# The mixer's heads between the steps of its projections on TensorE

## The chip, the cores and the metric

The kernel runs on one core of one Trainium2 chip. Its time is the device time of one launch in microseconds (us), the median over a few launches. The engines are TensorE (PE, with its weight loads as PEld), VectorE (DVE), ScalarE (ACT), GpSimd (POOL) and SyncE (SP, which issues the weight loads from memory). Each runs its own list of instructions strictly in order; semaphores order them against each other.

## The reference

Two transformer blocks on 512 tokens of width 1024 in fp32. The first block is a feed-forward part, a token mixer and a second feed-forward part, all scaled and shifted by a modulation vector; then come two layers with attention. The change touches the token mixer alone:

```python
def token_mix(y, w_in, conv_w, conv_b, gate_b, mnorm_g, lb, hnorm_g, w_out):
    p = y @ w_in                              # 1024 x 4104: mq mk mv mo | mif (8) | hq hf hi hg, 512 each
    mq, mk, mv, mo, mif, hq, hf, hi, hg = split(p)
    mq, mk = split(silu(causal_dwconv(concat(mq, mk), conv_w, conv_b)))    # 4 taps
    log_i, log_f = mif + gate_b, then log_sigmoid of the second half
    hm = mlstm_chunkwise(q, k, v, log_i, log_f)          # 4 heads of 128
    out_m = head_rmsnorm(hm, mnorm_g) * sigmoid(mo)
    fgate = lb + (1 - lb) * sigmoid(hf)
    ho = hgrn2_chunkwise(silu(hq), 1 - fgate, hi, log(fgate))              # 4 heads of 128
    out_h = head_rmsnorm(ho, hnorm_g) * silu(hg)
    return concat(out_m, out_h) @ w_out
```

`mlstm_chunkwise` is, per head, h = (W * (q k^T)) v over a normaliser, with W[t,s] = exp of differences of running sums of the gates, causal. `hgrn2_chunkwise` is a linear recurrence with a decay for each channel: o[t] = sum over s <= t of (q[t] * k[s] * decay(s..t)) summed over channels, times v[s].

## The kernel before

Activations lie feature-major: 128 features on the partitions, 512 tokens along the free axis. A product `y @ w` runs in **halves**: 128 output columns, 8 steps over the contraction (k), and 3 matmuls a step (`passes`), since both operands are split into a high and a low part of type fp32r: high by high, low by high, high by low. A half is thus 24 matmuls of 512 columns into one PSUM bank. The weights come in units of two halves through `raw` (2 slots, a `dma_start` on SP each). ACT copies a half to its high part (`split_hi`, into `wh`), DVE subtracts for the low part (`split_lo`, into `wl`); both run four halves ahead of PE. The products for `v` and `hi` are taken token-major instead (`token_major`), with 256 columns a matmul and one half for two halves' weights.

The mixer (`mix` on each engine) has three stretches:

1. The input product: 17 units, 33 tiles (the unit `if` has 8 columns), in the order of the table `MIX`. ACT evicts each tile and applies silu or sigmoid on the way; for q and k it copies to SBUF (`tmpB`), DVE convolves there and ACT applies silu.
2. The heads. First the four mLSTM heads ("M" below). For each key tile j: PE makes scores (L1736), DVE the argument of the weights from a row that PE has spread over the partitions (L1730, L1251), ACT their exponential (L794), POOL the causal edge (L569), DVE the product (L1258), PE values and row sums (L1747, L1749). At the head's end come an exponential and an absolute value on ACT, a maximum, a reciprocal (L1264) and a product on DVE, then a square on ACT, a mean over the head on PE (`head_stat`, L1696), a reciprocal root on ACT, gain and gate on DVE, and the split into high and low parts. Then the four HGRN heads ("H"): running sums (L1191), and for each of nine **levels** a subtraction on DVE (L1301), two exponentials on ACT (L812, L813), two products into `pair` on DVE (L1313, L1314), 4 matmuls of 128 columns on PE (L1769) and a masked copy of their result on DVE (L1284). The matmuls of the heads are plain fp32, and the profile shows two records for each.
3. The output product: 4 units, 8 halves over the eight head outputs, which all must be there first (`product`).

The attention layers further on are already written in another manner: PE's list takes steps of a product (a generator `beside`) between the matmuls of the attention, a fixed number at each place (`more(n)`).

## Time and profile before

| | us |
|---|---|
| Median of 3 runs | 2939.34 (2937.59 to 2943.41) |
| The profiled execution, its own time | 2942.35 |
| Its span, first to last instruction | 2940.5 |
| PE busy in the span | 2608.4 (89%) |
| DVE, ACT, POOL busy | 1417.3, 979.2, 216.1 |
| Mixer: input product | 493 to 677 |
| Mixer: heads | 677 to 951 |
| Mixer: output product | 951 to 997 |

Busy time is read with the granted clock of TensorE beside it (PEclk, 1.00 is 2.4 GHz and 0.50 is 1.2 GHz): matmuls at the lower level take twice as long and make PE look busier than its work is. A matmul's duration contains its way through the array, which overlaps the next one; what one costs in a row of them is the distance between two starts.

### The profile page before, as it was taken

Reading aid. Unit: us, or ns where it says so; the run is one execution under the profiler, and the core shown is the slowest. Engines: PE = TensorE matmul, PEld = TensorE weight load, DVE = VectorE, ACT = ScalarE, POOL = GpSimd, SP = SyncE. Lnnn points to the kernel's source line nnn. Section 1 sums busy time; section 2 is a strip of 40 time slices with the busy share of each in tenths; the row PEclk is TensorE's granted clock in tenths of the full one; section 3 lists DMA queues with packets and bytes.
Section 4 is the critical chain, followed back from the end, with each engine's and each line's share of the span. In section 5 each row is a group of like instructions: output and inputs, shape, how many; then the busy total and the mean of one; then the engine's idle time right before and its main releaser. Section 6 shows DMA issues by size and latency. Waiting matters only on the chain. (4 is left out here: it accounts for less than half of the span.)

```text
span 2940.5 us, 28742 instructions
## 1 busy us (share of the span) xinstructions
PE 2608.4 (89%) x11468; PEld 2035.1 (69%) x11468; DVE 1417.3 (48%) x2200; ACT 979.2 (33%) x1515; POOL 216.1 (7%) x199
## 2 busy tenths in 40 slices
PE   2899898996656899999898899999799988999997
PEld 1788786883344688887676678888576545788875
DVE  5676524524555433322544375532655553755325
ACT  2322224332222432323333433322434443333233
POOL 0000110000000100001200110001210002000011
PEclk9999999997666999999999999999999998999999
DMA  8365423650000132322222123322132101333221
GB/s 286 126 194 193 148 90 58 90 111 30 0 0 0 43 113 89 100 90 83 84 82 78 44 86 101 100 97 95 61 99 68 56 29 43 101 100 101 97 83 57
DMA packets 229204, 257.73 MB, mean 88 GB/s; under 512 B 7208, under 2 KB 218664, under 8 KB 229072
## 3 DMA queue, kind: packets, MB, share of 16 engines
q1 hardware_dynamic: 218624, 221.30, 25.0%
q0 software_dynamic: 8672, 31.43, 3.4%
q10 hardware_dynamic: 1776, 3.18, 0.3%
q8 instruction: 91, 1.49, 0.2%
q14 instruction: 41, 0.34, 0.0%
HBM read 251.66 MB, written 2.62 MB: 86 GB/s over the span
## 5 line engine op out<-in xcount | busy, mean ns | idle before, releaser
L1049 DVE TENSOR_TENSOR wl<-raw,wh 128x1024 fp32r<-128x1024 f32 (+1 forms) x398 | 478.3, 1205 | 1024.7 <-ACT wh L616 1024.0
L1586 PE MATMUL G<-yh,wh 128*128 128x512 f32 x1928 | 776.9, 403 | 61.1 <-DVE yl L1079 26.0
L616 ACT ACTIVATE wh<-raw 128x1024 fp32r<-128x1024 f32 (+1 forms) x398 | 412.1, 1038 | 1106.4 <-PE G L1586 1067.4
L1586 PE MATMUL G<-yl,wh 128*128 128x512 f32 x1928 | 758.5, 393 | 0.0
L1586 PE MATMUL G<-yh,wl 128*128 128x512 f32 x1928 | 758.1, 393 | 0.0
L1586 PEld LDWEIGHTS G<-yh,wh 128*128 128x128 f32 x1928 | 367.0, 190 | 169.9 <-issue 54.3
L1586 PEld LDWEIGHTS G<-yl,wh 128*128 128x128 f32 x1928 | 366.2, 190 | 78.6
L1586 PEld LDWEIGHTS G<-yh,wl 128*128 128x128 f32 x1928 | 366.9, 190 | 77.3 <-issue 4.2
L1586 PE MATMUL G<-hidh,wh 128*128 128x512 f32 x704 | 280.7, 399 | 0.0
L1586 PE MATMUL G<-hidl,wh 128*128 128x512 f32 x704 | 278.9, 396 | 0.0
L1586 PE MATMUL G<-hidh,wl 128*128 128x512 f32 x704 | 278.8, 396 | 0.0
L512 POOL TENSOR_TENSOR acc<-acc,tmpC 128x512 f32<-128x512 f32 x86 | 148.0, 1721 | 961.8 <-ACT tmpC L622 961.8
L1586 PEld LDWEIGHTS G<-hidh,wl 128*128 128x128 f32 x704 | 132.9, 189 | 32.7 <-issue 1.0
L1586 PEld LDWEIGHTS G<-hidh,wh 128*128 128x128 f32 x704 | 132.9, 189 | 32.5 <-issue 1.0
L1586 PEld LDWEIGHTS G<-hidl,wh 128*128 128x128 f32 x704 | 132.7, 189 | 32.0
L692 ACT ACTIVATE hidh<-tmpA 128x512 fp32r<-128x512 f32 x88 | 55.6, 632 | 215.6 <-DVE tmpA L1146 215.6
L1586 PE MATMUL G<-wh,yh 128*128 128x256 f32 x384 | 114.2, 297 | 0.9 <-DVE aq L1334 0.9
L1586 PE MATMUL G<-wl,yh 128*128 128x256 f32 x384 | 108.7, 283 | 0.0
L1586 PE MATMUL G<-wh,yl 128*128 128x256 f32 x384 | 108.7, 283 | 0.0
L1769 PE MATMUL X<-pair 128*128 128x128 f32 x224 | 53.6, 416 | 53.2 <-DVE pair L1314 52.8
L1149 DVE TENSOR_TENSOR hidl<-tmpA,hidh 128x512 fp32r<-128x512 f32 x88 | 60.9, 693 | 61.4 <-ACT hidh L692 61.4
L1769 PEld LDWEIGHTS X<-pair 128*128 128x128 f32 x224 | 46.5, 308 | 60.0 <-issue 51.8
(263 smaller groups left out, 2929.4 us busy)
## 6 DMA issues: line engine op xcount, KB each, us to landing
raw<-in_ffn_w_in SPq DMA_DIRECT2D x44, 1024.0 KB, 5.1
raw<-in_ffn_w_gate SPq DMA_DIRECT2D x22, 1024.0 KB, 5.4
raw<-in_ffn_w_up SPq DMA_DIRECT2D x22, 1024.0 KB, 5.4
ada_c<-in_ada_w POOLq DMA_DIRECT2D x22, 1024.0 KB, 5.6
raw<-in_ffn_w_down SPq DMA_DIRECT2D x16, 1024.0 KB, 5.0
raw<-in_w_in SPq DMA_DIRECT2D x16, 1024.0 KB, 9.6
raw<-in_ffn_w_out SPq DMA_DIRECT2D x16, 1024.0 KB, 5.0
raw<-in_na_w_qkv SPq DMA_DIRECT2D x12, 1024.0 KB, 5.1
```

The source lines that it names most:

```text
L512: nc.gpsimd.tensor_tensor(acc[:, :], acc[:, :], C2[:, n % 2, :], ALU.add)\
L616: nc.scalar.activation(place(wh), src, ACT.Copy).then_inc(hi, 1)
L692: nc.scalar.activation(hidh[:, 2 * j + i, :], A2[:, i, :], ACT.Copy).then_inc(hidh_ready, 1)
L1049: nc.vector.tensor_tensor(place(wl), src, f32(place(wh)), ALU.subtract).then_inc(lo, 1)
L1149: nc.vector.tensor_tensor(hidl[:, 2 * j + i, :], A2[:, i, :], f32(hidh[:, 2 * j + i, :]), ALU.subtract).then_inc(hid_ready, 1)
L1586: ins = nc.tensor.matmul(bank, a, b, start=first and i == 0, stop=last and i == 2)
L1769: ins = nc.tensor.matmul(bank[:, c], a, b, start=True, stop=True)
```

## The change

The heads move from a stretch of their own in between the steps of the two products. The heads' work is cut into 64 **slots**: an H head has 10, an M head 5, in the order H0 H1 M0 M1 H2 H3 M2 M3, and 4 slots follow the last head. ACT, DVE and PE each walk the same table `SLOTS`. In a slot of an H head, PE takes 4 steps of a product (12 matmuls) and one level; in a slot of an M head, 4 steps, one score matmul, and one key tile's values. From slot 54 on fewer steps are left. What ends a head (`finish`, table `FIN`) lies in the up to four slots behind it. The columns of the input product are reordered (`MIX`), so that the first H heads' columns come first: 6 halves run before slot 0, 27 beside slots 0 to 53, and the first two halves of the output product, taken head by head, from slot 54 on; its other 6 follow as before. The weight splits and evictions of a half stand in every second slot (`block_behind`). Every head writes its values to bank G2 and the products use G0 and G1.

The convolution reads the PSUM bank directly (`conv`), in four operations on DVE with the bias in the first, and no copy by ACT goes ahead of it. The gates' and activations' silu and sigmoid are taken in place in five batches (`batched`, at slots 9, 24, 39, 49 and 55), since each change of function set needs an ACT_TABLE_LOAD; the gating of the head outputs is held back to slots 50 to 63 (`GATE_SLOT`).

```diff
-        MIX = (("q", 0), ("q", 1), ("k", 0), ("k", 1), ("v", 0), ("v", 1), ("if", 0),
-               ("hf", 0), ("hf", 1), ("hq", 0), ("hq", 1), ("hi", 0), ("hi", 1),
-               ("mo", 0), ("mo", 1), ("hg", 0), ("hg", 1))
+        MIX = (("hf", 0), ("hq", 0), ("hi", 0), ("q", 0), ("k", 0), ("v", 0), ("if", 0), ("hf", 1), ("hq", 1),
+               ("hi", 1), ("q", 1), ("k", 1), ("v", 1), ("hg", 0), ("hg", 1), ("mo", 0), ("mo", 1))
...
+        HEADS = (("H", 0), ("H", 1), ("M", 0), ("M", 1), ("H", 2), ("H", 3), ("M", 2), ("M", 3))
+        SLOTS = []
+        FIN = {}
+        for z, (kind, x) in enumerate(HEADS):
+            for i in range(LEVELS + 1 if kind == "H" else TT + 1):
+                SLOTS.append((z, kind, x, i))
+            for f in range(4):
+                FIN.setdefault(len(SLOTS) + f, []).append((z, kind, x, f))
+        SLOTS += 4 * [(8, "", 0, 0)]
+        BESIDE = [b for b in range(6, 34) if b != 13]
...
+        GATE_SLOT = {50: ("H", 0), 51: ("H", 1), 52: ("H", 2), 53: ("H", 3), 56: ("M", 0), 57: ("M", 1),
+                     59: ("M", 2), 63: ("M", 3)}
+        O_ORDER = list(GATE_SLOT.values())
...
+                def block(b, kind, half, t, g):
+                    if kind not in ("v", "hi"):
+                        split_hi(b + 4)
+                    if kind == "if":
+                        split_hi(b + 5)
+                    if kind in "qk":
+                        return
+                    act.wait_ge(done, b + 1)
+                    bank, c = G[BANK[g]], 2 * half + t
+                    if kind in ("v", "hi"):
+                        token_rows(mv if kind == "v" else hv, half, t, g)
+                        if t:
+                            split_hi(b + 3)
+                            split_hi(b + 4)
...
+                def batched(s):
+                    if s == 9:
+                        evicted(act, mix_of("k", 0))
+                        evicted(act, mix_of("k", 1))
+                        todo = [(mqk[:, n, :], ACT.Silu) for n in (0, 4, 1, 5)]
+                    elif s == 24:
+                        todo = [(hk[:, 2, :], ACT.Sigmoid), (hk[:, 3, :], ACT.Sigmoid), (hq[:, 2, :], ACT.Silu),
+                                (hq[:, 3, :], ACT.Silu)]
...
+                    for ap, fn in todo:
+                        ins = nc.scalar.activation(ap, ap, fn)
+                    ins.then_inc(batch, 1)
+                    log_and_exp()
...
+                for s, (z, kind, x, i) in enumerate(SLOTS):
+                    if i == 0:
+                        for of in FIN.get(s, ()):
+                            finish(*of)
+                    if kind == "H" and i < LEVELS:
+                        level_exp(x, i + 1)
+                    if kind == "M" and i < TT:
+                        weight_exp(x, i)
+                    if i:
+                        for of in FIN.get(s, ()):
+                            finish(*of)
+                    if block_behind(s):
+                        block(*block_behind(s))
...
+                def conv(b, n, g):
+                    dve.wait_ge(done, b + 1)
+                    w = vec[:, VOFF["conv_w"] + 4 * n:VOFF["conv_w"] + 4 * n + 4]
+                    bias = vec[:, VOFF["conv_b"] + n:VOFF["conv_b"] + n + 1]
+                    bank = G[BANK[g]]
+                    st.do(nc.vector.tensor_scalar(mqk[:, n, :], bank[:, :], w[:, 3:4], bias, ALU.mult, ALU.add))
+                    for d in (1, 2):
+                        st.do(nc.vector.scalar_tensor_tensor(mqk[:, n, d:S], bank[:, 0:S - d], w[:, 3 - d:4 - d],
+                                                             mqk[:, n, d:S], ALU.mult, ALU.add))
+                    nc.vector.scalar_tensor_tensor(mqk[:, n, 3:S], bank[:, 0:S - 3], w[:, 0:1], mqk[:, n, 3:S],
+                                                   ALU.mult, ALU.add).then_inc(gfree[BANK[g]], 1)
...
+                for s, (z, kind, x, i) in enumerate(SLOTS):
+                    fins = FIN.get(s, ())
+                    if i == 0 and s and HEADS[z - 1][0] == "H":
+                        for of in fins:
+                            finish(*of)
+                        fins = ()
+                    if kind == "H":
+                        if i:
+                            level_mul(x, i)
+                        elif z:
+                            level_sums(z, x)
+                        if i < LEVELS:
+                            level_sub(x, i + 1)
                         if i == 1:
...
+                            if z:
+                                dve.wait_ge(nd_mm, z)
+                            st.do(nc.vector.memset(attD, 0.0))
+                        if i:
+                            level_copy(x, i - 1)
+                    if kind == "M":
+                        if i < TT:
+                            weight_arg(x, i)
+                        if i:
+                            weight_scores(z, x, i - 1)
+                    for of in fins:
+                        finish(*of)
+                    if block_behind(s):
+                        block(*block_behind(s))
+                    rows(s)
+                    if s == 25:
+                        dve.wait_ge(batch, 2)
+                        forget_gate(2)
+                        forget_gate(3)
+                    if s in GATE_SLOT:
+                        gate_o(s)
+                    if s - 1 in GATE_SLOT:
+                        low_o(s - 1)
...
+            def beside_mixers():
+                for x in BESIDE:
+                    b, kind, g = b0 + x, MIX[x // 2][0], mix_tile(x // 2, x % 2)
+                    if kind in ("v", "hi"):
+                        yield from token_major_steps(b, g, x % 2, yh, yl)
+                        continue
+                    pe.wait_ge(lo, b + (2 if kind == "if" else 1))
+                    bank_free(pe, g)
+                    for k in range(KT):
+                        ins = passes(G[BANK[g]][:, :], wh[:, b % 4, k, :], wl[:, b % 4, k, :], yh[:, k, :],
+                                     yl[:, k, :], k == 0, k == KT - 1)
+                        if k == KT - 1:
+                            ins.then_inc(done, 2 if kind == "if" else 1)
+                        yield
+                b, g = BB["mixo"], TB["mixo"]
+                for n, (kind, x) in enumerate(O_ORDER):
+                    k = o_tile(kind, x)
+                    pe.wait_ge(o_ready, n + 1)
+                    for i in range(2):
+                        s = (b + i) % 4
+                        if n == 0:
+                            pe.wait_ge(lo, b + i + 1)
+                            bank_free(pe, g + i)
+                        ins = passes(G[BANK[g + i]][:, :], wh[:, s, k, :], wl[:, s, k, :], moh[:, k, :], mol[:, k, :],
+                                     n == 0, n == KT - 1)
+                        if n == KT - 1:
+                            ins.then_inc(done, 1)
+                        yield
...
+                for s, (z, kind, x, i) in enumerate(SLOTS):
+                    n = 2 if s < 54 else 1 if s < 62 else 0
+                    if kind == "H":
+                        more(2 * n)
+                        level(x, i)
+                    elif kind == "M":
+                        if i == 0:
+                            pe.wait_ge(batch, 3 if x >= 2 else 1)
+                            if x:
+                                pe.wait_ge(em_ready, x)
+                            else:
+                                pe.wait_ge(uT_ready, 1)
+                            gate_row(x, mo[0:4, 3, :]).then_inc(mb_mm, 1)
+                        if i < TT:
+                            scores(x, i)
+                        more(n)
+                        if i >= 2:
+                            ins = values(z, x, i - 2)
+                        more(n)
+                        if i == TT:
+                            values(z, x, TT - 1).then_inc(nd_mm, 1)
+                            gate_row(x, mrow[0:4, :]).then_inc(mt_mm, 1)
...
-            product("mixo", 3, 8, yh, yl)
+            product("mixo", 3, 8, moh, mol, 2)
```

How the lists stand. PE before, at the end of the M heads and through one H head (X and G are PSUM banks, `pair` the operands of a level, `att` the finished weights):

```order
L1753 MATMUL X<-pair,cst 128x512
L1696 MATMUL G<-tmpC,onesH 128x512
L1769 MATMUL X<-hq,hk 128x128 x4
L1769 MATMUL X<-pair 128x128 x28
L1772 MATMUL X<-pair 128x128 x2
L1776 MATMUL X<-pair 128x256 x2
```

PE after, at the end of slot 0 and the start of slot 1 of the first H head (L1771 are the three matmuls of a product step):

```order
L1771 MATMUL G<-yh,wh 128x512
L1771 MATMUL G<-yh,wl 128x512
L1771 MATMUL G<-yl,wh 128x512
L1949 MATMUL X<-hq,hk 128x128 x4
L1771 MATMUL G<-yh,wh 128x512
```

Levels that followed each other directly now have 12 product matmuls ahead of each.

DVE before, two levels of an H head (subtraction, two products, masked copy):

```order
L1301 TENSOR_TENSOR tmpC<-tmpB 128x512
L1313 TENSOR_TENSOR pair<-hk,tmpC 128x128x2
L1314 TENSOR_TENSOR pair<-hq,tmpC 128x128x2
L1284 COPY_PREDICATED att<-lev,X 128x512
L1301 TENSOR_TENSOR tmpC<-tmpB 128x512
L1313 TENSOR_TENSOR pair<-hk,tmpC 128x64x4
```

DVE after, slot 2 of the first H head and the start of slot 3 (L1161 is the low part of a weight half, L1312 to L1316 the convolution):

```order
L1360 TENSOR_TENSOR pair<-hk,tmpC 128x128x2
L1361 TENSOR_TENSOR pair<-hq,tmpC 128x128x2
L1347 TENSOR_TENSOR tmpC<-tmpB 128x512
L1371 COPY_PREDICATED att<-lev,X 128x512
L1161 TENSOR_TENSOR wl<-raw,wh 128x1024
L1312 TENSOR_SCALAR mqk<-G,vec 128x512
L1314 SCALAR_TENSOR_TENSOR mqk<-G,vec,mqk 128x511
L1314 SCALAR_TENSOR_TENSOR mqk<-G,vec,mqk 128x510
L1316 SCALAR_TENSOR_TENSOR mqk<-G,vec,mqk 128x509
L1360 TENSOR_TENSOR pair<-hk,tmpC 128x64x4
```

The masked copy has moved behind the subtraction, and in every second slot a weight half's low part, and in eight slots a convolution, stand between one level's subtraction and its products.

ACT after, slots 24 and 25 (L881 a batch, L663 the return to the exponential's set, L844 and L845 the end of head M0, L834 the weights of M1):

```order
L781 ACTIVATE hv<-G 128x2x256
L881 ACT_TABLE_LOAD
L881 ACTIVATE hk<-hk 128x512 x2
L881 ACT_TABLE_LOAD
L881 ACTIVATE hq<-hq 128x512 x2
L663 ACT_TABLE_LOAD
L844 ACTIVATE rstd<-X 128x512
L845 ACTIVATE tmpA<-G 128x512
L834 ACTIVATE tmpC<-tmpB 128x512
```

The end of a head waits on ACT behind three table loads and four activations.

## Rows read from the trace of the kernel before

**Rows 1.** Busy time of each engine by stretch: three mixer stretches, one attention layer.

```profile
core 0: us, PE busy (x) PEld busy (x) DVE busy (x) ACT busy (x) POOL busy (x), PEclk, DMA share, GB/s
493.00:677.00 184.00, 183.93 (x984) 159.47 (x983) 69.28 (x81) 69.60 (x92) 0.00 (x0) 0.99 0.53 92
677.00:951.00 274.00, 155.04 (x480) 102.56 (x480) 149.72 (x266) 65.90 (x138) 4.67 (x16) 0.63 0.01 4
951.00:997.00 46.00, 45.97 (x194) 37.34 (x194) 8.58 (x7) 14.86 (x21) 12.23 (x7) 0.97 0.23 69
2180.00:2436.00 256.00, 226.76 (x983) 144.12 (x984) 138.25 (x323) 102.62 (x219) 3.22 (x6) 0.93 0.16 52
```

**Rows 2.** PE in order of time (start, duration): last input and first output matmul.

```profile
676.54 0.39 PE L1586 MATMUL G<-yl,wh 128*128 128x512 f32 x1
...
951.03 0.80 PE L1586 MATMUL G<-yh,wh 128*128 128x512 f32 x1 [4.34 <-DVE yl L1183]
```

**Rows 3.** PE in order of time: one level's four matmuls at the upper clock.

```profile
823.56 1.05 PE L1769 MATMUL X<-hq,hk 128*128 128x128 f32 x8
```

**Rows 4.** PE in order of time, second attention layer: product steps and fp32 matmuls.

```profile
2206.22 0.39 PE L1586 MATMUL G<-yh,wl 128*128 128x512 f32 x1
...
2207.83 0.39 PE L1586 MATMUL G<-yl,wh 128*128 128x512 f32 x1
2208.15 1.13 PE L1967 MATMUL X<-ak,aq 64*128 64x512 f32 x4
2209.21 0.50 PE L1586 MATMUL G<-yh,wh 128*128 128x512 f32 x1
...
2213.54 3.70 PE L1986 MATMUL G<-PT,av 128*128 128x512 f32 x8 [0.84 <-ACT PT L892]
```

**Rows 5.** DVE in order of time: the cadence of two levels.

```profile
841.00 0.72 DVE L1284 COPY_PREDICATED att<-lev,X 128x512 f32<-128x512 uint8 x1
841.61 0.68 DVE L1301 TENSOR_TENSOR tmpC<-tmpB 128x512 f32<-128x512 f32 x1
843.08 0.43 DVE L1313 TENSOR_TENSOR pair<-hk,tmpC 128x256 f32<-128x256 f32 x1 [0.79 <-ACT tmpC L813]
843.42 0.42 DVE L1314 TENSOR_TENSOR pair<-hq,tmpC 128x256 f32<-128x256 f32 x1
```

**Rows 6.** ACT in order of time: the exponentials between them.

```profile
842.32 0.42 ACT L812 ACTIVATE tmpC<-tmpC 128x256 f32<-128x256 f32 x1 [2.03 <-DVE tmpC L1301]
842.64 0.40 ACT L813 ACTIVATE tmpC<-tmpC 128x256 f32<-128x256 f32 x1
```

**Rows 7.** Groups by line and form (busy, mean ns), 600 to 1150 us.

```profile
L1049 DVE TENSOR_TENSOR wl<-raw,wh 128x1024 fp32r<-128x1024 f32 x47 | 57.6, 1225 | 173.5 <-ACT wh L616 173.5
...
L616 ACT ACTIVATE wh<-raw 128x1024 fp32r<-128x1024 f32 x47 | 49.8, 1059 | 151.1 <-PE G L1586 136.3 <-DMA raw<-in_w_in 14.8
...
L1191 DVE TENSOR_TENSOR_SCAN tmpB<-ones,hf 128x512 f32<-128x512 f32 x4 | 4.8, 1200 | 0.0
...
L1251 DVE TENSOR_SCALAR tmpB<-X,uT 128x512 f32<-128x512 f32 x4 | 3.0, 746 | 2.2 <-PE X L1730 2.2
...
L1258 DVE SCALAR_TENSOR_TENSOR att<-X,tmpC 128x512 f32<-128x512 f32 x4 | 2.8, 692 | 4.5 <-PE X L1736 4.5
```

**Rows 8.** PE in order of time: the last matmul before the end of head M0.

```profile
701.83 1.12 PE L1753 MATMUL X<-pair,cst 4*128 4x512 f32 x2
```

**Rows 9.** DVE in order of time: the end of head M0.

```profile
704.89 3.35 DVE L1264 RECIPROCAL tmpB<-tmpB 128x512 f32<-128x512 f32 x1
...
715.35 0.69 DVE L1183 TENSOR_TENSOR yl<-tmpA,yh 128x512 fp32r<-128x512 f32 x1 [0.70 <-ACT yh L736]
```

**Rows 10.** ACT in order of time: a table load and what follows.

```profile
605.92 1.28 ACT L776 ACT_TABLE_LOAD   x1
607.22 0.60 ACT L776 ACTIVATE hq<-G 128x512 f32<-128x512 f32 x1
```

**Rows 11.** Landing times of the 18 loads of the input product's weights.

```profile
DMA to landing us min/median/max: 6.2/8.9/19.6
```

More of the change, by code:

```diff
@@ L778, in mix, with token_rows @@
-                log_and_exp()
-                act.wait_ge(row_x, 1)
-                st.do(nc.scalar.activation(C2[0:4, 0, :], pair[0:4, 1, :], ACT.Abs))
-                st.do(nc.scalar.activation(C2[0:4, 1, :], C2[0:4, 0, :], ACT.Exp, scale=-1.0))
-                nc.scalar.activation(C2[0:4, 1, :], C2[0:4, 1, :], ACT.Ln, bias=1.0).then_inc(row_l, 1)
-                for t in range(NH):
+                def token_rows(dst, half, t, g):
+                    to = dst[:, 2 * t:2 * t + 2, half * UC:(half + 1) * UC]
+                    nc.scalar.activation(to, G[BANK[g]][:, :].rearrange("p (a c) -> p a c", a=2), ACT.Copy)\
+                        .then_inc(gfree[BANK[g]], 1)
@@ new lines, in mix @@
+                for b in range(6):
+                    kind, half = MIX[b // 2]
+                    g = TB["mix"] + b
+                    if kind == "hi":
+                        block(b0 + b, kind, half, b % 2, g)
+                    else:
+                        split_hi(b0 + b + 4)
+                        act.wait_ge(done, b0 + b + 1)
+                        to, fn = (hk, ACT.Sigmoid) if kind == "hf" else (hq, ACT.Silu)
+                        nc.scalar.activation(to[:, b % 2, :], G[BANK[g]][:, :], fn).then_inc(gfree[BANK[g]], 1)
+                    if b == 3:
+                        log_and_exp()
+                        log_f(0)
+                        log_f(1)
@@ L1234, in mix, with forget_gate @@
-                all_evicted(dve, TB["mixo"])
-                for t in range(NH):
+                def forget_gate(t):
                     st.do(nc.vector.tensor_scalar(hf[:, t, :], hk[:, t, :], lbc[:, 1, t:t + 1],
@@ L1792, in mix, with gate_row, scores @@
                     ins.then_inc(nd_mm, 1)
-                    head_stat(NH + x)
+                def gate_row(x, row):
+                    return nc.tensor.matmul(X[1][:, :], ident[0:4, x:x + 1].broadcast_to([4, P]), row,
+                                            start=True, stop=True)
+                def scores(x, j):
+                    n = TT * x + j
+                    if n in (0, 1, 8, 9):
+                        pe.wait_ge(lv_c, (19, 20, 39, 40)[n % 2 + n // 4])
+                    else:
+                        pe.wait_ge(s_ready, n - 1)
+                    nc.tensor.matmul(X[2 + n % 2][:, 0:S - P * j], mqk[:, NH + x, P * j:P * (j + 1)],
+                                     mqk[:, x, P * j:S], start=True, stop=True).then_inc(sc_mm, 1)
@@ new lines, in values @@
+                def values(z, x, j):
+                    pe.wait_ge(s_ready, TT * x + j + 1)
+                    if j == 0:
+                        pe.wait_ge(ho_ready, z)
+                        if x:
+                            pe.wait_ge(em_ready, x)
+                        else:
+                            evicted(pe, g0 + 3)
+                        for t in range(2):
+                            evicted(pe, mix_of("v", x // 2 * 2 + t))
+                    nc.tensor.matmul(G[2][:, P * j:S], mv[:, j, DH * x:DH * (x + 1)], att[:, j, P * j:S],
+                                     start=j == 0, stop=j == TT - 1)
+                    return nc.tensor.matmul(G[3][:, P * j:S], ones[:, :], att[:, j, P * j:S],
+                                            start=j == 0, stop=j == TT - 1)
@@ L1795, in root_column @@
+                for _ in side:
+                    pass
             def root_column():
```

589 lines of the change are left out of this document (311 added, 278 removed).

## The prediction

> **What bounds the kernel now.** I read first the page's 40 slices: PE is busy at the full clock nearly everywhere, and PEclk falls to 6 in three slices that follow each other. The busy time by stretch puts these in the mixer's heads [rows 1]: 274 us in which PE is busy for 155 at a mean clock of 0.63, DVE for 150, ACT for 66. The reader is to see there that no engine is full. Next to it the input product: 184 us with PE busy throughout at 0.99, while DVE and ACT work for 69 and 70 us. The heads lack PE work, the products have DVE and ACT to spare. Third I read PE in order of time, for the edges [rows 2]: the last input matmul starts at 676.54, the first output matmul at 951.03, 274.1 us after the end of the other at 676.93. Fourth, the cadence of a level on DVE and ACT [rows 5, 6].
>
> The bound moves: PE bounds the products; in the heads a chain over DVE, ACT and PE does. In the changed kernel both share the slots, so each slot costs the larger of PE's work and DVE's chain.
>
> **What goes.** The stretch of the heads: 274.1 us.
>
> **What PE gets instead.** No product step is added or removed. A product matmul costs 0.23 us from start to start (2206.22 to 2207.83 is seven of them, [rows 4]; with the next digit 0.227), a step of three 0.68. The heads' matmuls in plain fp32 now run at the upper level of the clock. One level of four took 1.05 us there with its way through the array [rows 3], so 0.95 in a row of others. Four of 512 columns took 3.54 us [rows 4], 0.89 each, and fewer columns take their share.
> - H head: 8 levels x 0.95, the two wide ones 0.5 and 0.9, values of 1280 columns 2.2, the mean 0.9: 12.1 us.
> - M head: two gate rows 1.8, scores 2.2, values and sums 4.4, the mean 0.9: 9.3 us.
> - Going between products and fp32 matmuls: in [rows 4] the scores stand between 2207.83 and 2209.21, 1.38 us for 1.06 of scores and 0.23 of the last product matmul, and the first product matmul after them is 0.1 longer. I take 0.15 a change: 12 in an H head, 8 in an M head.
>
> That is 4 x 13.9 + 4 x 10.5 = 97.6 us. If nothing else waited, the heads would cost 97.6 in place of 274.1.
>
> **What of DVE's chain sticks out.** PE's slot in an H head is 4 x 0.68 + 0.95 + 0.15 = 3.8 us, 7.7 for two. On DVE [rows 5], the subtraction starts at 841.61 and the products at 843.08: 1.47 us, filled by the two exponentials [rows 6] and two handovers; the products take 0.68. The masked copy (0.62) now lies inside the 1.47. So a slot without a weight half costs DVE 2.15 us. In one with a half, ACT copies the high part behind the exponentials (0.40 after the start of L813, then 1.04), DVE takes the low part (1.17) [rows 7]: 0.68 + 2.47 + 1.17 = 4.3. Two slots make 6.45, less than 7.7: **these are PE's**. A convolution adds four operations out of PSUM: one like L1251 (0.75) and three like L1258 (0.69) [rows 7], 2.8 us, so 9.25 against 7.7: **these are DVE's**. Eight slots have one, four in H0, one in M1, three in H2. The copy of q and k that ACT loses costs nothing either way: ACT had 114 us idle in that stretch.
> An M slot needs 1.9 us of DVE and a share of splits against 4.7 of PE, and PE runs two key tiles ahead: nothing sticks out there but the ends. In order of the slots:
> - H0: 4 x 1.55, less the start that DVE has ahead of PE: 3 us.
> - H1: five pairs 32, running sums 2.6 (1.2 for the long one [rows 7], 1.4 estimated for four of a quarter of its length), the end of H0 2, the fill 0.5, the gate rows 6 (each on 4 partitions, yet as long as on 128), 43 with a wait for PE's transposed row against PE's 41.5: 3 us.
> - M0 to M1: PE stands before M1's first matmul until ACT has taken two functions of the end of M0, 1.2 us and handovers, and these lie behind a batch of 3 x 1.28 + 4 x 0.6 us [rows 10]: 3 us. M2 to M3, without a batch: 2 us.
> - H2: three convolutions 4.7; its running sums (2.6) and M1's reciprocal with the products around it (3.35 + 1.3, [rows 9]) ahead of its first level: 7. Together 12 us.
> - M3: the batch at slot 55 (5 us on ACT) stands between its exponentials, DVE waits for it with the first M gate, and PE has only two steps a slot: 5 us.
> - After M3: from the last gate row to the low part of the head's output it took 14.2 us for M0 (701.83 to 716.04, [rows 8, 9]); 0.9 less at full clock, 2.7 us of product steps beside it: 10 us. This is what became of the 9 us with which the heads ended before.
> - The clock after that gap: as before the output product, six matmuls at 0.43, counted above already; 1 us more.
> - Loads: a unit has 6 slots (23 us) to land, 4 where two halves are split at once (15 us); landing took 8.9 in the middle and 19.6 at most [rows 11]: ACT would wait up to 4 us in one or two places, with its exponentials behind it: 3 us.
> - Uneven slots: the attention layer with the same manner of list had PE busy 227 of 256 us [rows 1], most of the loss at its end. I take 5 us.
>
> Together 47 us, bounded below by 13 (the end alone) and above by 97, if every slot with a half were as long as one with a convolution.
>
> Here a rule weighs against the change. [rows 10] show a load of 1.28 us with the next function starting 0.02 us behind it. The Trainium skill (ScalarE: Activation LUTs, "What ACT_TABLE_LOAD costs") gives every switch a further drain of some 1.38 us. The changed list has 11 loads in the slots, five of them where PE waits; by the rule these would cost an estimated 7 us more and the time would be 2817 us. The trace disagrees, so I leave it out.
>
> **Sum.** 274.1 - 97.6 - 47 = 129.5 us less. The profiled execution took 2942.35, which gives 2812.9; it lay 3.0 above the median of the runs, so the median to expect is 2810.
>
> **The rivals.**
> 1. PE bounds every slot. For it: DVE's 219 us of both stretches and ACT's 136 [rows 1], some of it outside the slots, are less than PE's 255 us in the slots, and DVE may run a slot ahead of PE. Against it: the sums for H0 and H2, and the ends of M heads in strict order. Only the 13 us at the end stay: 163.5 less, 2776.
> 2. ACT and DVE hold each other up more than I counted. ACT's list has evictions that wait for PE ahead of exponentials; if each of the 27 halves delayed the chain by one eviction and handover more (0.6 + 0.3) and the batches came out whole (5 x 5 us), stalls would be 96 us: 80 less, 2859. Against it: a half is done a slot before its eviction is due.
> 3. The engines go in step: PE's level waits for DVE's products and DVE's for PE's last level, so that each of the 40 H slots costs PE's 3.8 and DVE's 2.15 us in turn. The code has two buffers of `pair` and asks for the level before last, which speaks against it. 86 us in place of the 18 counted for H: 61 less, 2878.
> 4. Slower: the clock stays at the lower level in the slots. The heads ran at 0.63 with PE busy 155 of 274 us, the attention layer at 0.93 with 227 of 256 [rows 1]; H0 and H2 would have PE at work about 80% of the time. At 1.2 GHz throughout, the 158 us of product steps take 297, the heads' 98 take 190, and with 34 before, 13 of end and 33 behind the mixer takes 567 us against 504: 63 more, 3003. It would need a mean clock under 0.61 in the slots.
> 5. The interleaving doesn't happen, since some wait of PE runs behind a whole head: time as before, 2939. The list of PE's instructions speaks against it.
>
> **How the numbers follow.** Forecast (stalls of 30 to 65 us) 0.60, rival 1 0.15, rival 2 0.17, rival 3 0.04, rival 4 0.02, rival 5 0.01, the rest spread. The predicted time is the forecast's, 2810. The range takes in rival 1 and most of rival 2: 2774 to 2858. Within 0.2%, about 6 us and what a measurement here can tell from no change, only rival 5 lies: 0.01. Faster 0.96, slower 0.03.
>
> **What the changed profile would show.** Right: no stretch with PEclk 6 left; PE at work nearly without a gap from 493 to about 750, with a mean clock above 0.9; level matmuls at about 0.95 us a group; DVE between a subtraction and its products 1.47 us with the masked copy inside; PE waiting for DVE's products in slots behind convolutions, for ACT's absolute value before M1 and M3, and about 10 us before the last head's steps; the mixer's end near 868. Wrong: PE waiting in ordinary H slots, by which rival 2 or 3 is told (an idle engine behind `pair` in 40 places); a granted clock below 0.8 in the slots; ACT waiting for the loads for more than 10 us; or stalls so few that the mixer ends before 840.

## The result, and the profile after

The changed kernel takes 2808.2 us (2806.4 to 2809.4, 4 runs) against 2939.2 (2937.6 to 2943.4) for the kernel before on the same chip: a ratio of 0.955, 95% interval 0.9539 to 0.9562. 131 us are gone; 2810 was forecast. The profiled execution took 2808.76, its span is 2807.0.

First the clock and the engines, from the page after. PEclk is the granted clock in tenths:

```profile
PE 2563.0 (91%) x11468; PEld 2006.7 (71%) x11468; DVE 1415.8 (50%) x2198; ACT 988.4 (35%) x1527; POOL 216.1 (8%) x199
...
PEclk9899999999989999999998999999999989999999
```

No slice with a 6 is left. The work is the same for DVE and ACT; PE is busy for 45 us less, because the heads' matmuls, which ran at a mean clock of 0.63, now run beside product steps at 0.83 to 1.00. The busy time by stretch stands against [rows 1]; in order the lines are the six halves ahead of slot 0, H0, H1, M0, M1, H2, H3, M2, M3, the end of M3, and the output product:

```profile
core 0: us, PE busy (x) PEld busy (x) DVE busy (x) ACT busy (x) POOL busy (x), PEclk, DMA share, GB/s
493.00:527.70 34.70, 34.70 (x192) 30.51 (x193) 18.35 (x27) 20.39 (x27) 0.00 (x0) 0.96 0.61 79
527.70:572.60 44.90, 40.28 (x219) 34.80 (x219) 35.99 (x60) 14.74 (x29) 0.00 (x0) 0.92 0.34 53
572.60:617.80 45.20, 41.86 (x241) 35.66 (x239) 35.03 (x61) 21.16 (x39) 0.00 (x0) 0.98 0.36 71
617.80:650.60 32.80, 29.62 (x141) 21.97 (x141) 8.38 (x14) 14.41 (x21) 1.17 (x4) 0.86 0.16 38
650.60:677.00 26.40, 26.40 (x103) 18.53 (x103) 19.55 (x28) 7.98 (x13) 1.17 (x4) 0.89 0.21 40
677.00:725.00 48.00, 40.17 (x243) 35.32 (x244) 38.27 (x60) 19.87 (x36) 0.00 (x0) 0.96 0.29 52
725.00:765.40 40.40, 39.19 (x208) 32.91 (x207) 28.62 (x51) 20.46 (x37) 0.00 (x0) 1.00 0.24 70
765.40:793.00 27.60, 24.59 (x99) 17.07 (x98) 14.24 (x22) 11.72 (x19) 1.54 (x4) 1.00 0.23 76
793.00:813.00 20.00, 19.91 (x60) 12.24 (x60) 11.83 (x17) 10.25 (x16) 1.46 (x4) 0.83 0.00 1
813.00:827.00 14.00, 4.55 (x10) 2.62 (x10) 7.32 (x7) 3.66 (x6) 0.00 (x0) 0.76 0.00 0
827.00:866.00 39.00, 38.31 (x154) 29.73 (x153) 8.58 (x7) 16.44 (x24) 12.24 (x7) 0.96 0.25 81
```

Two losses are read from such a line: PE's idle time (length less PE busy) and what the lower clock costs ((1 - PEclk) x length at most, and never more than half of PE busy). The mixer's last product matmul starts at 863.88 where it started at 996.68; these 132.8 us are nearly all of the 133.5 by which the spans differ. Next, what PE waited for in the mixer (total us, times, longest):

```profile
PE X L1949 <- DVE pair L1361: 12.4, 6, 3.6
PE X L1881 <- ACT acc L848: 8.3, 2, 7.1
PE X L1982 <- ACT tmpA L845: 4.2, 2, 2.9
PE X L1956 <- DVE pair L1361: 3.3, 1, 3.3
```

Of 36 levels on `pair` (L1949, L1952 and L1956 for the last two of a head) only seven kept PE waiting. The cadence of two levels in H1, PE in order of time, against [rows 3]:

```profile
589.50 1.06 PE L1949 MATMUL X<-pair 128*128 128x128 f32 x8
590.31 0.48 PE L1771 MATMUL G<-yh,wh 128*128 128x512 f32 x1
...
593.15 1.06 PE L1949 MATMUL X<-pair 128*128 128x128 f32 x8
```

From level to level it is 3.65 us. Twelve product matmuls at 0.227 are 2.72, and a level's four matmuls of 128 columns, priced from the 0.89 of one with 512 [rows 4], are 0.89 more; that leaves 0.04 for going from one kind to the other and back. H3 has the same distance. In what follows a level counts as 3.65 less 2.72, 0.93. In H0 DVE sets the pace, in order of time on DVE, against [rows 5]:

```profile
536.61 0.68 DVE L1347 TENSOR_TENSOR tmpC<-tmpB 128x512 f32<-128x512 f32 x1
537.21 0.74 DVE L1371 COPY_PREDICATED att<-lev,X 128x512 f32<-128x512 uint8 x1
539.03 1.23 DVE L1161 TENSOR_TENSOR wl<-raw,wh 128x1024 fp32r<-128x1024 f32 x1 [1.08 <-ACT wh L654]
540.18 0.80 DVE L1312 TENSOR_SCALAR mqk<-G,vec 128x512 f32<-128x512 f32 x1
541.02 1.53 DVE L1314 SCALAR_TENSOR_TENSOR mqk<-G,vec,mqk 128x511 f32<-128x511 f32 x2
542.58 0.75 DVE L1316 SCALAR_TENSOR_TENSOR mqk<-G,vec,mqk 128x509 f32<-128x509 f32 x1
543.25 0.42 DVE L1360 TENSOR_TENSOR pair<-hk,tmpC 128x256 f32<-128x256 f32 x1
543.58 0.42 DVE L1361 TENSOR_TENSOR pair<-hq,tmpC 128x256 f32<-128x256 f32 x1
543.91 0.69 DVE L1347 TENSOR_TENSOR tmpC<-tmpB 128x512 f32<-128x512 f32 x1
...
546.07 0.69 DVE L1347 TENSOR_TENSOR tmpC<-tmpB 128x512 f32<-128x512 f32 x1
```

A slot with a half and a convolution costs DVE 7.30 us (536.61 to 543.91), one without 2.16: 9.46 for two, against 7.30 on PE. What such a lag leads to is seen on PE at the end of H1:

```profile
614.69 1.28 PE L1956 MATMUL X<-pair 128*128 128x256 f32 x4 [3.30 <-DVE pair L1361]
...
624.52 0.63 PE L1771 MATMUL G<-yh,wh 128*128 128x512 f32 x1
...
626.03 0.40 PE L1771 MATMUL G<-yh,wl 128*128 128x512 f32 x1
```

After 3.30 us of waiting (the slice 614.6 to 618 has a mean clock of 0.64, 618 to 622 one of 0.50) the product matmuls stand 0.43 apart until 625.8, then 0.23. The wait cost 3.3 us, and the lower level behind it up to 5.1 more (0.36 x 3.4, 0.50 x 4 and, with a clock of 0.53 from 622 to 626, 0.47 x 4). It isn't so behind every wait. The next lines are PE's windows behind the wait of 2.86 us before M1's first gate row, and behind one of 3.27 in H2 that ends at 709.47:

```profile
650.60:653.00 2.40, 2.40 (x3) 0.90 (x4) 0.32 (x1) 0.00 (x0) 0.00 (x0) 0.50 0.00 0
653.00:656.00 3.00, 3.00 (x10) 1.97 (x10) 2.97 (x3) 0.63 (x1) 0.29 (x1) 0.50 0.00 0
656.00:660.00 4.00, 4.00 (x25) 3.54 (x25) 3.93 (x7) 0.28 (x1) 0.00 (x0) 0.94 0.02 4
...
709.40:713.00 3.60, 3.53 (x30) 3.53 (x31) 3.33 (x8) 1.52 (x5) 0.00 (x0) 1.00 0.70 172
```

The first is followed by 5.9 us at the lower level, the second by none. And the end of M3, where nothing is left to put beside it (PE, ACT and DVE in order of time; [rows 8, 9]):

```profile
812.00 1.12 PE L1982 MATMUL X<-mrow,cst 4*128 4x512 f32 x2
815.05 3.35 DVE L1416 RECIPROCAL tmpA<-tmpA 128x512 f32<-128x512 f32 x1
820.25 2.08 PE L1881 MATMUL X<-acc,onesH 128*128 128x512 f32 x2 [7.14 <-ACT acc L848]
825.99 0.69 DVE L1459 TENSOR_TENSOR mol<-mo,moh 128x512 fp32r<-128x512 f32 x1 [0.69 <-ACT moh L926]
826.74 0.49 PE L1771 MATMUL G<-moh,wh 128*128 128x512 f32 x1 [2.31 <-DVE mol L1459]
```

### The profile page after: what moved, and what is told of

It reads as the page before. It is cut to its first block and busy times, and to the rows that moved or that the text cites. A ratio compares the mean times of both kernels' runs of the same rounds, so it can differ in the third digit from the quotient of the medians.

```text
span 2807.0 us, 28803 instructions
## 1 busy us (share of the span) xinstructions
PE 2563.0 (91%) x11468; PEld 2006.7 (71%) x11468; DVE 1415.8 (50%) x2198; ACT 988.4 (35%) x1527; POOL 216.1 (8%) x199
## 5 line engine op out<-in xcount | busy, mean ns | idle before, releaser
L1161 DVE TENSOR_TENSOR wl<-raw,wh 128x1024 fp32r<-128x1024 f32 (+1 forms) x398 | 478.0, 1205 | 946.1 <-ACT wh L654 945.5
L1771 PE MATMUL G<-yh,wh 128*128 128x512 f32 x1864 | 760.2, 408 | 56.4 <-DVE yl L1191 25.5
L1771 PE MATMUL G<-yl,wh 128*128 128x512 f32 x1864 | 734.4, 394 | 0.0
L1771 PE MATMUL G<-yh,wl 128*128 128x512 f32 x1864 | 733.9, 394 | 0.0
L1771 PEld LDWEIGHTS G<-yh,wh 128*128 128x128 f32 x1864 | 355.8, 191 | 163.5 <-issue 56.8
L1771 PEld LDWEIGHTS G<-yh,wl 128*128 128x128 f32 x1864 | 355.8, 191 | 76.6 <-issue 5.9
L1771 PEld LDWEIGHTS G<-yl,wh 128*128 128x128 f32 x1864 | 354.4, 190 | 76.6
L1771 PE MATMUL G<-hidh,wh 128*128 128x512 f32 x704 | 280.7, 399 | 0.0
L1771 PE MATMUL G<-hidl,wh 128*128 128x512 f32 x704 | 278.9, 396 | 0.0
L1771 PE MATMUL G<-hidh,wl 128*128 128x512 f32 x704 | 278.8, 396 | 0.0
L1771 PEld LDWEIGHTS G<-hidh,wl 128*128 128x128 f32 x704 | 132.7, 189 | 33.0 <-issue 1.0
L1771 PEld LDWEIGHTS G<-hidh,wh 128*128 128x128 f32 x704 | 132.7, 189 | 32.8 <-issue 1.0
L1771 PEld LDWEIGHTS G<-hidl,wh 128*128 128x128 f32 x704 | 132.6, 188 | 32.3
L1771 PE MATMUL G<-wh,yh 128*128 128x256 f32 x384 | 117.9, 307 | 0.0
L1771 PE MATMUL G<-wl,yh 128*128 128x256 f32 x384 | 109.7, 286 | 0.0
L1771 PE MATMUL G<-wh,yl 128*128 128x256 f32 x384 | 109.7, 286 | 0.0
L996 ACT ACTIVATE pb<-pb,sm 128x512 f32<-128x512 f32 x64 | 45.7, 715 | 115.8 <-DVE sm L1636 115.8
L1771 PEld LDWEIGHTS G<-wh,yh 128*128 128x128 f32 x384 | 74.7, 194 | 8.1 <-issue 7.4
```

The costliest lines, as they stand in the source:

```text
L996: nc.scalar.activation(pb[:, c, :], pb[:, c, :], ACT.Exp, bias=sm[:, c:c + 1], scale=-1.0, accum_out=sm[:, 8 + c:9 + c]).then_inc(da_e, 1)
L1161: nc.vector.tensor_tensor(place(wl), src, f32(place(wh)), ALU.subtract).then_inc(lo, 1)
L1771: ins = nc.tensor.matmul(bank, a, b, start=first and i == 0, stop=last and i == 2)
```

## The experiments

The kernels were run in three groups of four, and the kernel before took 2939.4 us beside the first (conv_short, no_switch, level_one, recip_off), 2941.0 beside the second (conv_late, unbatched, recip_act, pool_low) and 2942.7 beside the last; so the ratios are compared as well. An interval is about 0.0015 to either side, 4 us, and the change has its own of 0.0011; a smaller difference is looked for in the trace. One trace is one execution, and its clock is not the same each time (shown at the end of the next section), so that a mark in it can stand 1 to 3 us off for that alone. The mark used there is the last gate row of M3 on PE (812.00 in the changed kernel, above).

**conv_short.** Is the convolution on DVE what keeps PE waiting? Three of its four operations are left out.

```diff
-  st.do(nc.vector.tensor_scalar(mqk[:, n, :], bank[:, :], w[:, 3:4], bias, ALU.mult, ALU.add))
-  for d in (1, 2): ...                                   # taps 2 and 3
-  nc.vector.scalar_tensor_tensor(...).then_inc(gfree[BANK[g]], 1)     # tap 4
+  nc.vector.tensor_scalar(mqk[:, n, :], bank[:, :], w[:, 3:4], bias, ALU.mult, ALU.add)\
+      .then_inc(gfree[BANK[g]], 1)
```

> Leaves out three of the four taps of the convolution: each of its eight places costs VectorE 0.8 us in place of 3.1. Theory (a slot costs the larger of TensorE's work and VectorE's chain): a pair of slots with a convolution is 9.5 us on VectorE against 7.3 on TensorE; without the taps it is 7.2. H0 and H2 lose their waits behind convolutions: 8 to 12 us less than 2808, so 2796 to 2800, and the waits for pair fall from about 15 to under 6 us. Rival (TensorE bounds the slots, and the waits there come from the clock): within 2 us of 2808. Rival (the convolutions cost all their time): 18 us less, 2790.

2792.2 us (ratio 0.950, 0.9486 to 0.9514): 16 less than the change. DVE was relieved of 8 times 2.35 us (the convolution of 3.07 us at 540.18 shrinks to 0.72), and most of the 18.8 comes back. PE's waits for `pair` in this kernel:

```profile
PE X L1952 <- DVE pair L1357: 3.3, 1, 3.3
...
PE X L1945 <- DVE pair L1357: 2.1, 2, 1.2
```

10.3 us of waits for `pair` went, and 16 of the time: a wait costs more than its length. In H0 and in H1 up to its last level no wait is left, and the granted clock is 1.00 from 527 to 604 us. H0's 4.6 us of waits went and, with them, the 3.6 at most that the lower clock cost there; M0's gate row comes at 609.50 for 618.12, M3's at 796.69 for 812.00. DVE is the bound of the convolution slots.

**pool_low.** The other way round: all the work is kept, but the low parts of the seven halves behind convolutions move from DVE to POOL, which is idle there.

```diff
+  for q in {0: ON_POOL[:4], 8: ON_POOL[4:]}.get(n, ()):         # ON_POOL = (2, 4, 6, 8, 30, 32, 34), in POOL's list
+      ...
+      nc.gpsimd.tensor_tensor(place(wl), src, f32(place(wh)), ALU.subtract).then_inc(lo, 1)
```

> The low parts of the seven weight halves that VectorE takes beside convolutions in H slots go to GpSimd, which is idle there. It needs about 3.4 us for each (an estimate from 1.72 us for 512 elements), with six slots of time. Theory (VectorE's pair of slots with a convolution falls from 9.5 to 7.4 us, TensorE's is 7.3): 10 to 14 us less, 2794 to 2798, no wait for pair behind convolutions but in H2's first slot. Rival (VectorE and GpSimd slow each other while both work on SBUF): VectorE's operations beside them get longer and half of the gain or more is gone, 2801 or above.

2794.2 us (0.9497, 0.9479 to 0.9515): 14 less, at the upper end of what was expected. A low part takes 2.41 us on POOL, where 3.4 had been estimated, and the waits for `pair` fell from 15.7 us to 7.3. PE's level starts in H0 now lie 7.6 apart for two slots (541.26, 548.89, 556.52), where DVE's 9.46 stood.

**conv_late.** The same DVE work at other places: q and k ahead of hi in the table, so that their convolutions fall where DVE has less to do.

```diff
-  ("hi", 1), ("q", 1), ("k", 1), ("v", 1),
+  ("q", 1), ("k", 1), ("hi", 1), ("v", 1),
```

> The columns of q and k of heads 2 and 3 come before those of hi: the second four convolutions stand in slots 24, 26, 28 and 30 in place of 28, 30, 32 and 34, so two of them leave H2 for M heads, whose slots leave VectorE time. Theory (a convolution costs only in H slots, 2.2 us each and what the clock loses behind the wait): 4 to 7 us less than 2808, 2801 to 2804, no wait for pair in slots 33 and 35. Rival (a convolution costs wherever it stands): no change. Rival (VectorE has no room in M slots either, the waits move there): within 2 us of 2808.

2801.9 us (0.9525, 0.9507 to 0.9542): 6 less. Waits for `pair` on L1949 fell from 12.4 us to 7.9: in H2 only the first is left (3.33 us), and those in slots 33 and 35 are gone, as expected. M3's gate row comes at 807.83. Where a half's work falls matters, not only its sum.

**level_one.** Does PE bound any slot? From level 2 on only the first of the four matmuls is made; DVE's and ACT's work stays.

```diff
-  for t in range(TT):
+  for t in range(TT if i < 2 else 1):
```

> Of a level's four matmuls only the first runs in levels 2 to 7 (the masked copies still read the whole bank): 24 levels of 0.93 us on TensorE become 0.24, 16.6 us of its work. Theory (ordinary pairs of slots are TensorE's with 7.3 us, VectorE's chain of 6.3 to 6.5 lies right below): a pair can fall by 0.9 only, in H1 and H3, and hardly where convolutions stand: 5 to 9 us less, 2799 to 2803. Rival (TensorE bounds all slots): 16 us less, 2792. Rival (VectorE bounds all): no change, 2808.

2801.1 us (0.953, 0.9516 to 0.9544): 7 less, of about 16 us of matmuls taken away. The waits for `pair` rose in turn:

```profile
PE X L1949 <- DVE pair L1361: 20.1, 10, 3.9
```

Some of what is taken from PE is gained, in slots that PE bounds, and the rest turns into waits for DVE.

**recip_off and recip_act.** The reciprocal of 3.35 us stands in DVE's list four times. First one cheap operation in its place (the normaliser isn't inverted), then the same function by a logarithm and an exponential on ACT, one slot later.

```diff
-  st.step(nc.vector.reciprocal(o, o))
+  st.step(nc.vector.tensor_scalar(o, o, 1.0, None, ALU.mult))           # recip_off
+  st.do(nc.scalar.activation(o, o, ACT.Ln))                             # recip_act, ACT's list at f == 1
+  nc.scalar.activation(o, o, ACT.Exp, scale=-1.0).then_inc(rc_ready, 1)
```

> The reciprocal of each M head (3.35 us on VectorE, four of them) becomes a multiplication by one (0.43 us). Theory: M0's and M2's lie in slots of M heads, where VectorE has time to spare, and cost nothing; M1's stands ahead of H2's first level, M3's in the end that everything waits for: 2.9 us each, 6 us less, 2802. Rival (all four count): 12 us less, 2796. Rival (only the last counts, since TensorE has product steps to do in H2's first slots): 3 us less, 2805.

> The reciprocal of each M head goes from VectorE (3.35 us) to ScalarE as exp(-ln), 1.3 us and handovers, one slot later. Theory: the end after M3 gains 1.8 us, H2's first level about 1.5; 3 to 4 us less, 2804 to 2805. Rival (as with the reciprocal left out): 5 us less, 2803. Rival (ScalarE's two functions delay the exponentials of the slots where they stand): no change.

2803.2 us (0.9543, 0.9527 to 0.9559) and 2801.9 (0.9524, 0.9507 to 0.9542): 5 and 6 less, which the timing alone does not tell from each other; the ratio of recip_off by itself is not told from the change's 0.955 either. By the traces it is the same two places. The wait before H2's first level falls from 3.57 us to 1.24 and 1.22, and the later waits for `pair` in H2 take none of it back (4.1 us for 4.2; recip_act has a new wait of 0.7 for `acc`). At the end of M3 the wait is 4.3 and 5.1 for 7.1. (H2's first level starts even 4.1 and 4.5 us earlier, at 683.02 and 682.64 for 687.15, but 1.8 and 2.2 of that are there at M1's last gate row already, behind a shorter stretch of low clock, 3.4 us for 5.9.) The reciprocals of M0 and M2 show in no wait.

**no_switch.** What do the loads of function sets cost? All functions of the batches are taken from one set, which leaves out silu and sigmoid there and 11 loads.

```diff
-  ins = nc.scalar.activation(ap, ap, fn)
+  ins = ... ACT.Copy if fn == ACT.Silu else ACT.Exp, scale=0.0
-  log_and_exp()
```

> In the five batches silu becomes a copy and sigmoid an exponential of zero, so that none of the 11 table loads in the slots is there; the activations stay. Theory (a load costs ScalarE 1.28 us, and counts only where TensorE waits for ScalarE: at the end of M0 and in M3): 3 to 5 us less, 2803 to 2805. Rival (the Trainium skill, ScalarE: Activation LUTs, with a drain of 1.38 us behind each load, five of them in waits): 13 us less, 2795. Rival (all loads are hidden): no change, 2808.

2805.6 us (0.9546, 0.9532 to 0.9561): 2.6 less, within the uncertainty, where 3 to 5 were expected; neither that nor no change is ruled out. The wait before M1 and M3 fell from 4.2 us to 2.6, M3's gate row comes 1.0 earlier. In the changed kernel the load at 643.16 takes 1.28 us, and the function behind it starts at 644.46. The Trainium skill (ScalarE: Activation LUTs, "What ACT_TABLE_LOAD costs") gives a further drain of some 1.38 us for each switch. It is borne out neither by these rows nor by the 2.6 us, where the rival with the drain had 13.

**unbatched.** The opposite: no batches at the slots 24, 49 and 55, silu and sigmoid as each half is evicted, with a load before and behind each.

```diff
-  nc.scalar.activation(to, bank[:, :], ACT.Copy).then_inc(gfree[BANK[g]], 1)
+  nc.scalar.activation(to, bank[:, :], fn).then_inc(gfree[BANK[g]], 1)
+  log_and_exp()
```

> Undoes three of the five batches: silu and sigmoid of hf, hq, hg and mo are taken at the eviction, as in the kernel before, each with a table load ahead and one behind to return to the exponential; 24 loads where the batches had 7, 22 us more on ScalarE. Theory (ScalarE has idle time behind each weight half, the load pair moves the next exponential by 0.7 us only, inside TensorE's slack; and the wait before M1 and the stop in M3 lose their batch): 0 to 3 us less, 2805 to 2808. Rival (the batches are what makes the interleaving cheap; each of the 12 evictions delays a level by a load pair): 10 to 25 us more, 2818 to 2833.

2806.1 us (0.9541, 0.9522 to 0.9559): not told from the change, though the mixer has 31 loads in place of 14. The 17 further loads, 22 us more of ACT, lie beside PE's work but for one: the wait for the eviction ahead of M2's end (`hf`) is 3.2 us for 1.8, while the one before M1 fell from 2.9 to 1.3. These batches earn nothing that shows.

**before_conv.** The convolution out of PSUM by itself, put into the kernel before: ACT's eight copies go, one element is copied on DVE as a signal.

```diff
-  nc.scalar.activation(B2[:, t, 3:S + 3], bank[:, :], ACT.Copy).then_inc(gfree[BANK[g]], 1)
+  st.do(nc.vector.tensor_scalar(c, bank[:, :], w[:, 3:4], None, ALU.mult))
+  ...                                                                   # three more taps from the bank
+  dve.wait_ge(gfree[BANK[g]], ORD[g] + 1)
+  nc.vector.tensor_copy(sm[0:1, 0:1], c[0:1, 0:1]).then_inc(mconv, 1)
```

> One part of the change alone, in the kernel before: the convolution reads the PSUM bank, VectorE frees the bank, and ScalarE's eight copies go. Theory (the input product is TensorE's there, with VectorE and ScalarE at less than half): no change, 2937 to 2942. Rival (the change's gain has a share from this): at least 5 us less, 2934 or below.

2942.0 us against 2942.7 (0.9998, 0.9986 to 1.0009): nothing. ACT is busy 6 us less in the input product (63.6 for 69.6), beside a PE that bounds it. So the gain comes from the interleaving and not from this part.

**out_after.** The part with the output product: no step of it in slots 54 to 63, all four units after the heads.

```diff
-  n = 2 if s < 54 else 1 if s < 62 else 0
+  n = 2 if s < 54 else 0
-  product("mixo", 3, 8, moh, mol, 2)
+  product("mixo", 3, 8, moh, mol, 0)
```

> Undoes one part: the first two halves of the output product (16 steps, 10.9 us of TensorE) run after the last head, with the other six, and not between the slots of M2 and M3. Theory (in M3's slots half of the steps fill waits of TensorE behind ScalarE's batch and the gates): 3 to 8 us more, 2811 to 2816. Rival (they lay wholly in waits): 10 us more, 2818. Rival (TensorE bounds these slots, so it is the same work elsewhere): 1 us more, 2809.

2810.8 us (0.9547, 0.9534 to 0.956): 3 more by the times, not told from 0 by the ratios. The trace says why so little. From M3's first gate row to its last it takes 16.3 us (788.51 to 804.77) in place of 18.9: the ten steps that stand there, 6.8 us of PE, cost only 2.65. Without them PE waits in M3, and the clock is lower (0.69 for 0.82):

```profile
795.47 1.22 PE L1977 MATMUL X<-mqk 128*128 128x256 f32 x2 [3.03 <-DVE att L1399]
```

DVE's product `att` stands there behind M2's reciprocal (791.02 to 794.37). M2's end is 3.4 us shorter, for two steps and the wait of 1.8 us for `hf`. But the sixteen steps then follow behind the last wait, where the clock is low again (0.66 from 812 to 830), and the mixer ends 3.1 us later. So 4.2 us of the 6.8 are had for nothing in M3, out of waits and of the lower clock, much as the theory had it; what is left of that at the mixer's end is of the size of the uncertainty.

**pool_recip and best.** What the runs pointed to. pool_recip has the low parts of nine halves on POOL (also slots 16 and 18) and the reciprocal on ACT. best has in addition no late batches, and holds product steps back for the end of M3:

```diff
-  n = 2 if s < 54 else 1 if s < 62 else 0
+  n = 2 if s < 54 else 1 if s < 57 else 0
+  if s in (60, 61):
+      more(3)                     # ahead of the mean over M3's head
```

> The low parts on GpSimd as in pool_low, also for slots 16 and 18, where VectorE has the gate rows, and the reciprocal on ScalarE as in recip_act. Theory (the two gains lie at different places, H0 and H2 behind convolutions against the end and H2's start, and add): 2794 less 5 for the reciprocal and 2 to 3 for the wait in slot 19, 2784 to 2789. Rival (what is gained at one place is lost at the next wait, the gains overlap): 2791 or above.

> As pool_recip, with silu and sigmoid at the eviction as in unbatched, and with six product steps kept back from slots 57 to 59 and put into the wait after M3. Theory: TensorE stands 7 us there, six steps are 4.1 us; with the 2 us of unbatched that is 5 to 6 us less than pool_recip, 2777 to 2784. Rival (slots 57 to 59 are bound by M3's chain, and the steps there cost nothing already): 2 us less than pool_recip.

2789.0 us (0.9472, 0.9459 to 0.9485) and 2787.5 (0.947, 0.9457 to 0.9484, 5 runs). Both beat the change, by 19 and 21 us; pool_recip gives all but 1 of what pool_low and recip_act gave singly (14 + 6). best's additions give 1.5, not the 5 to 6 hoped for, not told from nothing; it misses its range. Its waits on PE at M2's end (`hf`) and behind M3, in an execution that took 2782.92, the fastest of the five:

```profile
PE G L1780 <- ACT hf L823: 3.2, 1, 3.2
PE G L1780 <- DVE mol L1467: 3.0, 1, 3.0
...
PE X L1890 <- ACT acc L864: 1.9, 2, 1.2
```

The wait for the square (`acc`) is filled, from 7.1 us to 1.2, but PE waits 3.0 for the low part where it waited 2.3 in the change and 1.8 in pool_recip, and 3.2 where it waited 1.8 for an eviction. The last is `hf`, which now has a load and a function in it, as in unbatched.

## Why the prediction was right

By its own steps:

- **The move of the bound** came as told: each slot costs the larger of PE's work and DVE's chain. level_one and conv_short show both kinds; rivals 3 (in step), 4 (the clock stays low) and 5 are out by the cadence of 3.65 us and the clock of 0.96 in H0 to H3 together, and rival 2 (held up by ACT) by unbatched and by only seven waits of PE in 36 levels. Rival 1 (PE bounds every slot, 2776) was wrong by the slots behind convolutions; with DVE relieved, pool_recip goes towards it (2789).
- **What PE gets, 97.6 us**, was too much by about 9. The mis-sized term is the 0.15 us for each of the 80 changes between products and fp32 matmuls, 12 us; it had been read from one pair of rows in [rows 4]. H3 and M2, where the clock is 1.00, show it: 68.0 us, less 4.2 idle and 173 product matmuls at 0.227 (39.3), leave 24.5 for the heads' matmuls. The forecast's prices for them are 23.6 without the changes, so that 20 changes cost 0.9 at most, 0.05 each. Over all heads that makes an estimated 89 us.
- **DVE's chain**: 9.25 forecast for two slots with a convolution, 9.46 measured. The first operation out of PSUM takes 0.80 for 0.75 and the three others 0.75 for 0.69. A pair without a convolution stays below PE's 7.30: no wait is seen there.
- **The stalls, 47 us**, were about 52. PE's idle time, and the loss to the clock by the windows above:

| | forecast | PE idle | clock, at most |
|---|---|---|---|
| H0 | 3 | 4.6 | 3.6 |
| H1 | 3 | 3.3 | 0.9 |
| M0, M1 | 3 | 3.2 | 7.5 |
| H2 | 12 | 7.8 | 1.9 |
| H3, M2 | 2 | 4.2 | 0 |
| M3 | 5 | 0.1 | 3.4 |
| end of M3 | 10 | 9.5 | 2.3 |
| clock, loads, unevenness | 1 + 3 + 5 | in the rows above | |
| sum | 47 | 32.7 | 19.6 |

89 + 32.7 + 19.6 is 141.3 us in place of the 274.1; the spans say 140.6, and the forecast said 144.6. So three terms were mis-sized and cancel in part: the changes of kind (about 9 too much); the idle time, forecast at up to 46 and measured at 32.7; and the clock, for which 1 us stood and up to 19.6 was lost. ACT waited for a weight load once, for 1.3 us, where 3 had been set aside. That 2810 and 2808.2 lie so close is luck in part: for the profiled execution the forecast was 2812.9, and it took 2808.76. The upper bound of 97 us doesn't follow from its own words either: 1.55 us more for each of the other 19 halves makes 76. A single microsecond for the clock ignored what [rows 2] already show behind a wait, a matmul at the lower level: after the change it falls behind the waits that end at 544.05 (to 547.2), 562.97, 614.69 (to 625.8), 650.60 (to 656.5), 687.15 (to 690.6), 793.09 (to 799.9), 820.25 and 826.74 (to 830.6).
- **The batch at slot 55** (5 us) was too much. PE has no idle time in M3: the product steps fill its waits (out_after), and the stretch is PE's work at a mean clock of 0.83; no_switch and unbatched bring 2.6 and 2 us, not told from nothing, and not there alone.
- **The end of M3**: 10 forecast from M0's end before, 9.5 of idle measured.
- **The drain behind a table load** that the Trainium skill has (ScalarE: Activation LUTs, "What ACT_TABLE_LOAD costs") was rightly left out, by no_switch and by the rows.

What stays open is when the clock falls. Behind waits that product steps follow it is low for 3 to 3.5 us (544.05, 687.15) or not at all (709.47); behind those that gate rows and scores of an M head follow, for 6 to 11 (614.69, 650.60, 793.09). In best it is low from 794.95 to 797.94, behind M3's last gate row at 793.0 and with only a wait of 0.65 ahead of that. That points to the gate rows and scores in plain fp32 as a part of it; no run changed these alone, so it isn't shown. Nor is it the whole of it, for the same wait before the same instructions isn't followed by the same clock in every execution. In no_switch the wait in H2 that left the clock at 1.00 above (709.47) is followed by 6.2 us at the lower level; in recip_off the one before M1 (650.60 above) by 3.4 in place of 5.9, starting later:

```profile
707.26 2.08 PE L1948 MATMUL X<-pair 128*128 128x128 f32 x8 [3.28 <-DVE pair L1360]
...
649.98 1.09 PE L1982 MATMUL X<-mo,cst 4*128 4x512 f32 x2 [2.86 <-ACT tmpA L845]
```

Neither run changed PE's list. So what a wait costs in clock can't be told from one trace, and the sum of up to 19.6 us is that of one execution too.

## What to carry to other kernels

Fill an engine's waits with another product's steps, and price each slot as the larger of the two engines' own work, with the handovers inside the longer chain; then look for the slots in which the filler itself loads the chain (here the convolution and the low part behind one half) and move that part to an idle engine, which was worth 14 us of 2808. Price a wait of the matmul engine at more than its length, for the clock behind it (here up to 19.6 us on 32.7). Merging table loads and taking copies from an engine with room were worth nothing that could be measured here; look for a wait on them first.

## What the runs showed of the hardware

- Plain fp32 and fp32r matmuls alternate at a loss of 0.05 us a change at most (24.5 us for 23.6 of work and 20 changes, in H3 and M2).
- POOL subtracts 128 x 1024 in 2.41 us where DVE takes 1.23. DVE beside it is slowed in one kind of operation only. From pool_low, POOL and DVE in order of time:

```profile
538.18 2.41 POOL L612 TENSOR_TENSOR wl<-raw,wh 128x1024 fp32r<-128x1024 f32 x1 [69.35 <-ACT wh L662]
539.30 0.75 DVE L1324 SCALAR_TENSOR_TENSOR mqk<-G,vec,mqk 128x509 f32<-128x509 f32 x1
539.96 0.91 DVE L1373 TENSOR_TENSOR pair<-hk,tmpC 128x256 f32<-128x256 f32 x1
540.79 0.41 DVE L1374 TENSOR_TENSOR pair<-hq,tmpC 128x256 f32<-128x256 f32 x1
```

The operations that read PSUM keep their 0.75; the product of two SBUF operands takes 0.91 in place of 0.42 and ends 0.28 us after POOL's end at 540.59, and again so at 547.58 (0.92, POOL's end at 548.22). The Trainium skill (SBUF — State Buffer, "SBUF: two separate sides") has such a DVE operation and a GpSimd one that reads SBUF exclude each other for a whole instruction. These rows agree; the half microsecond a time is in pool_low's result.
- A multiply-add of the convolution costs DVE as much out of PSUM as out of SBUF (0.75 us for 512 columns, as before). The first operation, a product with a scalar, doesn't: it takes 0.48 out of SBUF (kernel before, 512.01), 0.74 out of PSUM (before_conv), and 0.80 with the bias as a second scalar.
